# A transformer layer with routed experts: the last four expert tiles added to memory by column halves, and the last tile's down weights split earlier into other buffers

## The reference, cut to what matters

```python
def hier_moe(x, ...):            # x: 2048 prompt rows + 64 sample rows, D = 1024
    ...                          # top-1 of 4 groups, top-2 of its 4 experts -> gates
    hg = jnp.einsum('td,edf->tef', xt, w_gate)     # 16 experts, width 256
    hu = jnp.einsum('td,edf->tef', xt, w_up)
    act = jax.nn.silu(hg) * hu * gates[..., None]
    return jnp.einsum('tef,efd->td', act, w_down)
...
ffn = hier_moe(hn2, ...)
x = x + gt2 * rms_norm(ffn, p['g_post_ffn'])
```

## Time and profile before

| | |
|---|---|
| median of three runs | 1487.65 us |
| the profiled execution, its own time | 1486.71 us |
| its span, first to last instruction | 1484.9 us |
| PE busy | 1315.1 us, 89% |
| DVE busy | 1152.1 us, 78% |
| ACT busy | 815.5 us, 55% |
| POOL busy | 675.3 us, 45% |
| mean granted TensorE clock | 0.951 of full speed |

### The profile page before, as it was taken

One profiled execution on the slowest core, in us unless ns is written; L12 is line 12 of the kernel. 1 busy time (PEld: TensorE's weight loads), 2 busy tenths in 40 slices (PEclk: granted clock), 3 DMA queues, 4 the chain that ended last, 5 costly groups with the idle time before them and its releaser, 6 DMA issues. The chain is left out here.

```text
span 1484.9 us, 24502 instructions
## 1 busy us (share of the span) xinstructions
PE 1315.1 (89%) x7142; PEld 1028.7 (69%) x7142; DVE 1152.1 (78%) x2043; ACT 815.5 (55%) x1683; POOL 675.3 (45%) x760
## 2 busy tenths in 40 slices
PE   4999999989898989699999996399999999999930
PEld 2588888856565656488888885278888888888820
DVE  3788888837676778467666764989999999999937
ACT  2432333213345768434444442378898988889844
POOL 1107766832222890023222231346656576667615
PEclk9999999979999999899999998599999999999965
DMA  9423444469986654324444436756888988885789
GB/s 330 144 87 124 165 172 178 167 227 357 317 278 180 193 166 137 133 86 161 165 163 147 141 128 230 252 166 149 211 257 243 259 234 244 249 223 140 219 248 367
DMA packets 138879, 298.25 MB, mean 201 GB/s; under 512 B 22804, under 2 KB 80149, under 8 KB 136318
## 3 DMA queue, kind: packets, MB, share of 16 engines
q1 hardware_dynamic: 110982, 218.63, 42.7%
q0 software_dynamic: 20800, 61.13, 17.6%
q10 hardware_dynamic: 7024, 17.60, 3.3%
HBM read 305.18 MB, written 102.25 MB: 274 GB/s over the span
## 5 line engine op out<-in xcount | busy, mean ns | idle before, releaser
L2826 DVE TENSOR_TENSOR ex_w_lo<-route_wgu,ex_w_hi 128x1024 fp32r<-128x1024 f32 x192 | 225.8, 1217 | 3.4 <-ACT ex_w_hi L2634 1.8
L2634 ACT ACTIVATE ex_w_hi<-route_wgu 128x1024 fp32r (+1 forms) x192 | 193.1, 1064 | 4.0 <-issue 4.0
L2593 POOL DMA_INDIRECT scratch_acc<-route_o,ex_to x48 | 97.1, 2023 | 159.5 <-DMA scratch_acc<-route_o,ex_to 83.4
L147 PE MATMUL ex_ps_h<-ex_w_hi,ex_xT 128*128 128x512 f32 x384 | 155.4, 405 | 0.0
L148 PE MATMUL ex_ps_h<-ex_w_lo,ex_xT 128*128 128x512 f32 x384 | 151.8, 395 | 0.0
L2028 POOL TENSOR_SCALAR mx_st<-mx_st 128x1 f32<-128x1 f32 x68 | 38.7, 569 | 227.5 <-ACT mx_j L2076 127.2
L147 PE MATMUL fr_ps_m<-fr_whi,fr_hl 128*128 128x512 f32 (+1 forms) x384 | 138.7, 361 | 0.6 <-ACT fr_io L451 0.3
L149 PE MATMUL fr_ps_m<-fr_whi,fr_hl 128*128 128x512 f32 (+1 forms) x384 | 136.1, 354 | 0.0
L148 PE MATMUL fr_ps_m<-fr_wlo,fr_hl 128*128 128x512 f32 (+1 forms) x384 | 135.9, 354 | 0.0
L2863 DVE TENSOR_TENSOR ex_wd_lo<-route_wd,ex_wd_hi 128x1024 fp32r<-128x1024 f32 x96 | 114.8, 1236 | 5.7 <-ACT ex_wd_hi L2652 5.1
L2582 POOL TENSOR_SCALAR ex_eq<-ex_x,route_rc 128x2 f32<-128x2 f32 x48 | 114.5, 2386 | 0.1
(11 more groups left out here) (504 smaller groups left out, 3557.4 us busy)
## 6 DMA issues: line engine op xcount, KB each, us to landing
route_wgu<-in_w_exp_gate_dram SPq DMA_DIRECT2D x48, 1024.0 KB, 14.3
route_wgu<-in_w_exp_up_dram SPq DMA_DIRECT2D x48, 1024.0 KB, 15.6
route_wd<-in_w_exp_down_dram SPq DMA_DIRECT2D x48, 1024.0 KB, 13.9
scratch_rec<-fr_w SPq DMA_DIRECT2D x16, 1112.0 KB, 4.2
s_rec<-scratch_rec SPq DMA_DIRECT2D x32, 556.0 KB, 6.2
scratch_proj<-fr_io SPq DMA_DIRECT2D x16, 640.0 KB, 3.0
scratch_acc<-in_zeros_dram SPq DMA_DIRECT2D x18, 512.0 KB, 5.8
fr_w<-in_w_ada_dram SPq DMA_DIRECT2D x8, 1024.0 KB, 9.5
```

What stands on the lines that cost most here:

```text
L147: nc.tensor.matmul(out, hi, w_hi, start=first, stop=False)
L2593: pool.indirect_dma_start(T["acc"], bass.IndirectOffsetOnAxis(to[:, t:t + 1], 0), o[:, t % 2, :], None, compute_op=ALU.add).then_inc(sem(" ...
L2634: A(w_hi[:, par, c * PW:(c + 1) * PW], wgu[:, bass.ds(slot * (KD * 2 * DE) + c * PW, PW)], ACT.Copy).then_inc(S["w_rounded"], 1)
L2826: vec.tensor_tensor(w_lo[:, par, c * PW:(c + 1) * PW], wgu[:, bass.ds(slot * (KD * 2 * DE) + c * PW, PW)], w_hi[:, par, c * PW:(c + 1) * P ...
```

## The change

It does four things, all at the end of the expert stage.

1. The stores of tiles 44 to 47 become two each (`store_half`). `acc` is seen as rows of 512 columns, and a half's row is 2 x row + c; its index comes from a new small table `to_half`, which DVE computes with two instructions on 128x4 numbers in the routing part. Half c of a tile waits only for half c of the tile before.
2. The last step is written out in another order: `round_d` and `split_d` of tile 47 stand before its gate, and write to a free half of the gate and up weight buffers (`last_hi`, `last_lo`). Tile 47's rounded activations go to free room in `xT` (`last_a`).
3. `down` of tiles 46 and 47 is issued by halves, with `flip_a` of tile 47 between the halves of tile 46. A new semaphore `d_first` lets ACT copy tile 47's left half while the right one is computed.
4. Four and one of the `x2` loads are issued after `down_weights` of tile 47 and not before, and some tail buffers change places so that `last_hi` and `last_lo` are not overwritten.

```diff
+            def store_half(t, c):
+                at, n = slice(c * 512, (c + 1) * 512), t - BY_HALVES
+                pool.wait_ge(S["o_out_a"], t * 2 + 3 + c)
+                if n:
+                    pool.wait_ge(st_half[c], n * 16)
+                elif c == 0:
+                    pool.wait_ge(S["to_ready"], 3)
+                    pool.wait_ge(sem("st", (t - 1) % 2), ((t - 1) // 2 + 2) * 16)
+                pool.indirect_dma_start(acc_halves, bass.IndirectOffsetOnAxis(to_half[:, c, n:n + 1], 0), o[:, t % 2, at], None, compute_op=ALU.add).then_inc(st_half[c], 16)
...
-                store(t)
+                if t < BY_HALVES:
+                    store(t)
+                else:
+                    store_half(t, 0)
+                    store_half(t, 1)
...
@@ SP @@
-                if n == 2:
-                    load_x2_past(NTILE - 2, range(5, 9))
-                    load_x2_flipped(NTILE - 3, 10)
+            load_x2_past(NTILE - 2, range(5, 9))
+            load_x2_flipped(NTILE - 3, 10)
...
@@ ACT @@
-            gate(NTILE - 1, 1)
-            out(NTILE - 2, 0, HT - 1)
-            move_a(NTILE - 1)
-            round_d(NTILE - 1, U - 1, NTILE // U - 1, slot_of(NTILE - 1))
-            out(NTILE - 1, 1, HT - 1)
+            def out_half(t, c, done):
+                act.wait_ge(*done)
+                act.wait_ge(st_half[c], (t - 1 - BY_HALVES) * 16)
+                A(o[:, t % 2, c * 512:(c + 1) * 512], ps_o[:, c * 512:(c + 1) * 512], ACT.Copy).then_inc(S["o_out_a"], 1)
+
+            round_d(LAST_TILE, U - 1, NTILE // U - 1, slot_of(LAST_TILE), last_hi)
+            gate(LAST_TILE, 1)
+            move_a(LAST_TILE, last_a[0])
+            for c in range(2):
+                out_half(NTILE - 2, c, (S["d_done"], NTILE - 2 + NSL + 1))
+            out_half(LAST_TILE, 0, (S["d_first"], 1))
+            out_half(LAST_TILE, 1, (S["d_done"], LAST_TILE + NSL + 1))
...
@@ DVE @@
+            for c in range(2):
+                vec.tensor_scalar(to_half[:, c, :], none[:, BY_HALVES:], 2.0, c - 2.0, ALU.mult, ALU.add).then_inc(S["to_ready"], 1)
...
-            gate(NTILE - 1, U - 1)
-            split_d(NTILE - 1, slot_of(NTILE - 1))
+            split_d(LAST_TILE, slot_of(LAST_TILE), last_hi, last_lo)
+            gate(LAST_TILE, U - 1)
+            split_a(LAST_TILE, *last_a)
...
@@ PE @@
+            def down_half(t, c, hi=wd_hi, lo=wd_lo, a_hi=a_hi, a_lo=a_lo):
+                at = slice(c * 512, (c + 1) * 512)
+                pe.wait_ge(S["o_out_a"], t * 2 + c + 1)
...
-            gate_up(NTILE - 1, U - 1)
-            down(NTILE - 2)
-            flip_a(NTILE - 1)
-            down(NTILE - 1)
+            gate_up(LAST_TILE, U - 1)
+            ready(NTILE - 2)
+            down_half(NTILE - 2, 0)
+            flip_a(LAST_TILE)
+            down_half(NTILE - 2, 1).then_inc(S["d_done"], 1)
+            ready(LAST_TILE)
+            down_half(LAST_TILE, 0, last_hi, last_lo, *last_a).then_inc(S["d_first"], 1)
+            down_half(LAST_TILE, 1, last_hi, last_lo, *last_a).then_inc(S["d_done"], 1)
```

More of the change, by code:

```diff
@@ L2354 @@
 NSLOT = NTILE * P
+LAST_TILE = NTILE - 1
+BY_HALVES = NTILE - 4
 NSL = 3
@@ L2432, in moe @@
         x2_first, row5 = own("x2_first", at_xT, [P, D]), own("row5", at_row5, [P, 768])
-        x2_of = lambda t: x2_first[:, :] if t < 1 else wgu[:, (t + 3) * D:(t + 4) * D] if t < 9 else x[:, t - 9, 0:D] if t < 13 else spare_hi[:, t - 13, :]
+        x2_of = lambda t: x2_first[:, :] if t < 1 else wgu[:, (t + 3) * D:(t + 4) * D] if t < 9 else x[:, t - 9, 0:D] if t < 13 else spare_hi[:, t - 11, :] if t < 15 else spare_lo[:, t - 13, :]
         w5 = lambda k: wd[:, k * D:(k + 1) * D] if k < 6 else w5_rest[:, k - 6, :]
         bias5, gain5, c5 = row5[:, 0:256], row5[:, 256:512], row5[:, 512:768].rearrange("p (k n) -> p k n", k=KD)
+        to_half = s.sb("to_half", [P, 2, NTILE - BY_HALVES], U32)
+        last_hi, last_lo = (b[:, (NTILE - 2) % 2, 0:2 * D].rearrange("p (k n) -> p k n", k=2) for b in (w_hi, w_lo))
+        last_a = xT[1][:, 0:2, :], xT[1][:, 2:4, :]
         norm, eps = s.sb("norm", [P, NT, 3]), s.sb("eps", [P, 1])
-        f_of = lambda t: wgu[:, t * D:(t + 1) * D] if t < 4 else spare_hi[:, t, :] if t < 8 else spare_lo[:, t - 8, :] if t < 16 else wd[:, 2 * D:3 * D]
+        f_of = lambda t: wgu[:, t * D:(t + 1) * D] if t < 4 else spare_hi[:, t, :] if t < 8 else spare_hi[:, t - 8, :] if t < 10 else spare_lo[:, t - 10, :] if t < 12 else spare_lo[:, t - 8, :] if t < 16 else wd[:, 2 * D:3 * D]
         ps_gain, ps_f = (a[:, :, :].rearrange("p n d -> p (n d)") for a in (ps_t, ps_h))
@@ L2440, in moe @@
         names = ("G2_in G2_samples eps_set warm tailed hit tiled tiled_late numbered tail_out weighed wt_ready to_ready summed rooted rstd gained gain_moved y_pool g_ready y_ready y_out cleared5 consts5 w5_in mm5 mod5 row5 out5 ident_in step de exped hot counted planned matched turned rows_ready x_flipped x_moved_a x_moved_v w_rounded w_split d_rounded d_split a_split gu_done th_ready "
-                 "sg_ready a_ready a_flipped a_moved d_done o_out_a st_even st_odd").split()
+                 "sg_ready a_ready a_flipped a_moved d_first st_left st_right d_done o_out_a st_even st_odd").split()
         S = {n: s.sem(n) for n in names}
@@ L2456, in moe @@
             S["x2", t] = s.sem(f"x2_{t}")
-        HT = NTILE // 2
+        HT = BY_HALVES // 2
+        st_half = S["st_left"], S["st_right"]
+        acc_halves = T["acc"].rearrange("r (h d) -> (r h) d", h=2)
         LAST = NT - 1
@@ L2555, in _ @@
             sp.wait_ge(S["st_odd"], (HT + 1) * 16)
+            for landed in st_half:
+                sp.wait_ge(landed, (NTILE - BY_HALVES) * 16)
             for t in range(NT):
@@ L2609, in _ @@
                     refill(t + 2)
-                store(t)
+                if t < BY_HALVES:
[3 more added lines that the diff above has]
+                    store_half(t, 1)
             pool.wait_ge(S["st_even"], (HT + 1) * 16)
             pool.wait_ge(S["st_odd"], (HT + 1) * 16)
+            for landed in st_half:
+                pool.wait_ge(landed, (NTILE - BY_HALVES) * 16)
             for n, t in enumerate(BY_POOL):
@@ L2642, in gate, with move_a, round_d @@
                 A(th[:, :], ps_h[:, par, 0:DE], ACT.Tanh, scale=0.5).then_inc(S["th_ready"], 1)
-            def move_a(t):
+            def move_a(t, a_hi=a_hi):
                 act.wait_ge(S["a_flipped"], t + 1)
                 A(a_hi[:, :, :], ps_a[:, 0:2 * P].rearrange("p (k n) -> p k n", k=2), ACT.Copy, scale=0.5).then_inc(S["a_moved"], 1)
-            def round_d(t, n, q, slot):
+            def round_d(t, n, q, slot, hi=wd_hi):
                 act.wait_ge(S["d", n], q * 16 + 16)
                 for k in range(2):
-                    A(wd_hi[:, k, :], wd[:, bass.ds(slot * (2 * D) + k * D, D)], ACT.Copy).then_inc(S["d_rounded"], 1)
+                    A(hi[:, k, :], wd[:, bass.ds(slot * (2 * D) + k * D, D)], ACT.Copy).then_inc(S["d_rounded"], 1)
             def slot_of(t):
@@ L2856, in move_x, with split_a, split_d @@
                                       ALU.subtract).then_inc(S["x_moved_v"], 1)
-            def split_d(t, slot):
+            def split_a(t, a_hi=a_hi, a_lo=a_lo):
                 dve.wait_ge(S["a_moved"], t + 1)
                 vec.scalar_tensor_tensor(a_lo[:, :, :], ps_a[:, 0:2 * P].rearrange("p (k n) -> p k n", k=2), 0.5, a_hi[:, :, :].bitcast(F32), ALU.mult, ALU.subtract).then_inc(S["a_split"], 1)
+            def split_d(t, slot, hi=wd_hi, lo=wd_lo):
                 for k in range(2):
                     dve.wait_ge(S["d_rounded"], t * 2 + k + 1)
-                    vec.tensor_tensor(wd_lo[:, k, :], wd[:, bass.ds(slot * (2 * D) + k * D, D)], wd_hi[:, k, :].bitcast(F32), ALU.subtract).then_inc(S["d_split"], 1)
+                    vec.tensor_tensor(lo[:, k, :], wd[:, bass.ds(slot * (2 * D) + k * D, D)], hi[:, k, :].bitcast(F32), ALU.subtract).then_inc(S["d_split"], 1)
             def slot_of(t):
@@ L2890, in _ @@
             dve.wait_ge(S["out5"], 4 * 16)
+            split_a(0)
             split_d(0, slot_of(0))
@@ L2899, in step @@
                     split_w(t + 2, par, range(PARTS // 2), slot)
+                split_a(t)
                 split_d(t, own)
@@ L2974, in flip_a, with ready @@
                 last.then_inc(S["a_flipped"], 1)
-            def down(t):
+            def down_half(t, c, hi=wd_hi, lo=wd_lo, a_hi=a_hi, a_lo=a_lo):
+                at = slice(c * 512, (c + 1) * 512)
+                pe.wait_ge(S["o_out_a"], t * 2 + c + 1)
+                for k in range(2):
+                    last = three_products(nc, ps_o[:, at], a_hi[:, k, :], a_lo[:, k, :], hi[:, k, at], lo[:, k, at], k == 0, k == 1)
+                return last
+            def ready(t):
                 pe.wait_ge(S["a_moved"], t + 1)
@@ L2979, in down @@
                 pe.wait_ge(S["d_split"], t * 2 + 2)
[L2980 to L2985, removed]
+            def down(t):
+                ready(t)
```

(2 more changed lines are left out.)

## The result

| | before | changed |
|---|---|---|
| median, 20 runs each | 1487.92 us | 1489.86 us |
| the profiled execution's span | 1484.9 us | 1487.0 us |
| first split of tile 0's down weights to the first store | 7.05 us | 8.24 us |
| issue of store 43 to the last landing | 43.11 us | 43.85 us |
| last landing to the end | 48.38 us | 48.48 us |

The ratio is 1.0019, with a 95% interval of 1.001 to 1.0028: 1.5 to 4.2 us slower. It was forecast 2.2 us faster. The difference is under the 0.5% named as the bound of no change, but it is clear of its own interval and has the other sign.

What follows compares the result with a forecast made beforehand. Two chains, the last four stores and the compute behind them, were taken to bound the end together. Landing 2.4 us earlier, less 0.2 for the table, gave 2.2 us earlier, 1485.5 us; range 1482.0 to 1489.6.

Steps and rivals of the forecast that it cites:

- What bounds it: End of the expert stage: the chain of four stores and the compute chain arrive within 0.2 us of each other.
- Tile 47's weights ahead of its gate: Expert stage's end: costs tile 46 1.5 us, but takes the compute side off the path.
- Halves, undisturbed: Last stores: an undisturbed half lasts 4.8 us from issue to landing, against 6.0 for a whole store.
- Stores 44 and 45: Beside the x2 loads: halves last 5 to 9 us; tile 45 just in time, up to 1.5 us late.
- The loads beside tile 46: Tile 46's stores: the gain row takes 1.4 us of all engines, half of it charged, on the right half.
- forecast E of 40.7: Forecast stretch from the issue of store 43 to the last landing, in us.
- The table: Routing part, two instructions ahead of the plan: 0.2 us taken, 0.4 us at most.
- B: Rival, last stores: packets follow size, a half takes 4.3 us, tile 45 early; 4.6 us earlier, less 0.2; chance 0.20.
- C: Rival, last stores: an addition's packet costs 0.42 us whatever its size; 1.5 us later with the table; chance 0.15.
- D: Rival, stores beside loads: each half waits its own turn, some 3.4 us; 0.5 us earlier, less 0.2; chance 0.15.
- That the clock could cost anything: End of the stage: compute leaves the path, so PE's lower clock, 1.2 us later per half, costs nothing.
- The sums: Whole kernel: 2.4 - 0.2 = 2.2 us earlier, 1485.5 us; own range 1484.1 to 1486.8, chance 0.45.

Runs made afterwards that it cites:

- Experiment 4: The kernel before with only the half stores of tiles 44 to 47, ACT's waits by halves and the table; old compute order; 1.0009 of before.
- experiment 6: The kernel of experiments 5 with the gain row loaded earlier, into a free tail buffer; 0.999 of before.
- experiment 9: The kernel of experiment 6 with the table of half rows computed later, behind row 5 of the modulation; 0.9989 of before.
- experiment 1: The changed kernel with tile 0's slot number read ahead of both split_a and split_d; 0.9999 of before.
- experiments 5: The kernel of experiment 1 with the five x2 loads back ahead of tile 47's down weights; 1.0 of before.
- experiment 11: The changed kernel itself, measured again; 1.0007 of before.
- Experiment 10: The kernel of experiment 9 with half stores for tiles 46 and 47 alone, 44 and 45 stored whole; 1.0005 of before.
- experiment 3: The kernel of experiment 1 with whole stores for tiles 44 to 47 in place of halves; 1.0017 of before.
- experiment 7: The kernel of experiment 3 with the five x2 loads back where they were before; 1.0005 of before.
- experiment 2: The kernel before with tile 0's slot number read late, between the rest of the activations and the down weights' split; 1.0006 of before.

## Why the prediction was wrong

- **What bounds it**, two chains that arrive together: held. Experiment 4 shows the compute chain holding left 47 once the weights' split stays late.
- **Tile 47's weights ahead of its gate**: held to some 0.2 us, the 1.5 us loss on tile 46 included. The loss did no harm in the changed kernel, since left 46 waited for a landing anyway, and the gain was of no use: left 47 went at 37.06 us after store 43, where experiment 4, with the old compute order, let it go at 36.08. Only the versions with a shorter chain use it (35.05 in experiment 6, 34.41 in experiment 9).
- **Halves, undisturbed**: 4.8 us forecast, 4.93 and in experiment 1 4.70 measured. The row packet of 2 KB was taken as 0.27 us; in experiment 1 it is 79.0% of 5.0 us on 16 engines over 256 packets, 0.25 us:

```profile
q0 software_dynamic: 288, 0.52, 79.0%
```

- **Stores 44 and 45, "I take it as just in time"**: the step of the end that failed. Halves were to last 5 to 9 us beside the loads; left 44 took 11.20 and left 45 8.00. Left 46 was issued 29.83 us after store 43, forecast 27.5: 2.3 us. Left 45 came at 29.1, 1.5 us beyond the latest instant given for it (1421), once both are counted from store 43. Right 45 came at 32.2, where the sum needed 28.4.
- **The loads beside tile 46**: the gain row was charged at half of 1.4 us and on the right half alone, the moved `x2` loads at nothing here. Left 46 took 6.48 us, 1.7 more than forecast. By experiments 5 and 6 the gain row is 0.7 of that; the rest goes with the moved loads (0.65 to 1.0, one trace each). With 1.0 us regained, as right 47 followed its left by 1.86 us and not by 2.9, and 0.1 us more on right 47, these make up the 3.2 us between the forecast E of 40.7 and 43.85.
- **The table**: 0.2 us taken, 0.4 to 0.5 measured (A 25.87 to 26.34, and 26.27 back to 25.91), at the upper bound of 0.4.
- **The start of the loop**: no term at all. 0.44 us of DVE and 1.2 us of clock. The whole diff has the line, `split_a(0)` above `split_d(0, slot_of(0))`, and the cut one ahead of the prediction does not show it; I read it as a call cut in two that does the same. This and the table are 0.44 + 1.19 + 0.47 = 2.1 us, within the measured 1.5 to 4.2, with an end that on the mean of four executions (43.1) neither wins nor loses against 43.11 and 43.35. So the two steps that failed are this one, which gave the loss, and the one on stores 44 and 45, which with the loads beside tile 46 took away the forecast gain. That 2.1 lies so near the middle of the measured times is partly luck, since E alone moves by 1.3 us.
- **Rivals**: B (0.21 us a row packet) and C (0.42) are out by the packet time. D came nearest at the end, and its sign was met: it put right 45 at 31.6 us after store 43 and the last landing at 42.6, and measured were 31.6 to 32.2 and 42.5 to 43.85. In experiment 11 the chain even runs through the right halves, as D has it. But its mechanism, an own turn of some 3.4 us for each half, isn't what ran. Both halves of tile 45 were issued by 1418.34 in the changed kernel, and behind one empty stretch both queues moved equally many packets, from 1420.7 to 1425.7, with no empty stretch of its own for the second half:

```profile
q0 software_dynamic: 270, 0.52, 55.7%
q1 hardware_dynamic: 269, 0.97, 51.9%
```

  Nor was the empty stretch of the kernel before one share of 9 packets an engine: the 421 packets in it are 26 an engine. Experiment 10 contradicts D too, as left 45 came 2.8 us before a whole one, where D allowed 1. That the clock could cost anything was excluded for the end, rightly, and not asked for elsewhere.
- **The sums**: the forecast's own range, 1484.1 to 1486.8, does not follow from its words. Tile 45 late by 1.5 us gives 1487.0, and the lower end has no term.

Open: why tile 45 stored whole lands later in the new order, 31.3 to 31.4 us after store 43 in experiments 3, 7 and 10 against 29.6 and 29.8 in before and experiment 2. Part of it can be read: from 18 to 31 us after store 43 there ran 1035 plain load packets in experiment 3 (the moved loads) and 948 in experiment 10 (the gain row, issued early), against 784 in before and 801 in experiment 2. But experiment 7 has only 782 and is as late. No run separates this, and with so few executions part of it may be scatter.

## What to carry to other kernels

When a helper is cut in two, look at every call of it, also far from the place the change is about, and ask what was evaluated ahead of the first part and now stands between the two. Where PE already stands idle for some time, look at the clock granted behind it: here 0.44 us more on another engine cost 1.6. And two transfers that share a queue, an issuing engine and a loaded stretch are worth what the earlier landing of the first one lets start, less what else the freed time lets in, such as a load that used to sit in a gap.

## What was not expected of the hardware

A row packet of an addition to memory takes 0.42 us at 4 KB and 0.25 us at 2 KB, so 0.6 of the time for half the bytes. A wait of PE of 2.3 to 2.4 us at this place left its clock at 1.00 in eleven of eleven traces here, and one of 2.8 us was followed by 0.50 for some 3.4 us in three of three, each time only after PE had worked again for 1.5 us. And E differed by up to 1.3 us between executions of the same end code, as much as most of the edits were worth.
